# A second mixer with its order of work rewritten: scores ahead of a unit, convolution steps elsewhere, branch transposes spread out

## The reference, cut to what matters

```
proj = h @ w_in                       # 1024 x 7184: q, k, v, conv_in, gla_q/k/v/r, gla_lr, 3 x 1024 gates
sb_out   = stick_breaking_attention(q, k, v)      # 8 heads, 256 keys
   z = q k^T * scale;  log_keep = log_sigmoid(-z) on earlier keys
   w = exp(log_sigmoid(z) + reverse cumsum(log_keep) - log_keep);  out = w v
conv_out = silu(layer_norm(depthwise_conv_31(a * sigmoid(g)) + conv_b))   # 31 taps, 512 channels
gla_out  = rms_norm(gla_chunked(gla_q, gla_k, gla_v, log_alpha)) * silu(gla_r)
merged   = sum over the 3 branches of sigmoid(gate_b) * (branch_b @ w_branch[b])
out      = merged @ w_out
```

## Time and profile before

| | |
|---|---|
| median of 3 runs | 2477.34 us (2474.61 to 2477.43) |
| profiled execution | 2478.04 us, span of its instructions 2476.4 us |
| TensorE clock granted, mean | 0.97 of full speed |
| the mixers' stretches | from 1339 us on and from 2000 us on of the span |

### The profile page before, as it was taken

One profiled execution on the slowest core, in us unless ns is written; L12 is line 12 of the kernel. 1 busy time (PEld: TensorE's weight loads), 2 busy tenths in 40 slices (PEclk: granted clock), 3 DMA queues, 4 the chain that ended last, 5 costly groups with the idle time before them and its releaser, 6 DMA issues.

```text
span 2476.4 us, 38897 instructions
## 1 busy us (share of the span) xinstructions
PE 2310.3 (93%) x10840; PEld 1884.2 (76%) x10840; DVE 1754.4 (71%) x2364; ACT 1392.8 (56%) x1842; POOL 224.9 (9%) x291
## 2 busy tenths in 40 slices
PE   8988899998988899997999989999999998989998
PEld 6767788876776788875887777778878877777887
DVE  5767788886777788896556777665565559777555
ACT  4543677774653577774445555454454455654544
POOL 0000000000000000000000690000000009700000
PEclk9999999998999899998999999999999999999999
DMA  7433699994434699995665544555655554444652
GB/s 248 131 120 125 240 346 335 345 332 159 142 110 133 211 342 344 341 347 170 189 187 159 161 149 132 184 187 183 190 179 187 185 171 138 135 153 154 209 185 98
DMA packets 277483, 497.27 MB, mean 201 GB/s; under 512 B 20480, under 2 KB 112816, under 8 KB 277344
## 3 DMA queue, kind: packets, MB, share of 16 engines
q1 hardware_dynamic: 273296, 482.12, 58.2%
q0 software_dynamic: 4048, 13.50, 1.7%
HBM read 494.50 MB, written 1.05 MB: 200 GB/s over the span
## 4 chain that ended last, share of the span: by engine, by line
PE 72%; DVE 10%; DVEq 6%; ACT 4%; issue 4%; ACTq 1%; PEld 1%; DMA 1%; PEldq 0%; SPq 0%; POOLq 0%
PE g_bank L574 15%; PE g_bank L575 14%; PE g_bank L576 14%; PE s_bank L575 8%; PE s_bank L576 8%; PE s_bank L574 8%; DVE w_lo L563 2%; DVE conv_y L2456 2%; DVEq L2450 2%; ACT w_hi L558 1%; PE t_bank L1613 1%; PE t_bank L1757 1%; DVEq L2091 1%; DVE xt_lo L630 1%; DVE soft L2499 1%
## 5 line engine op out<-in xcount | busy, mean ns | idle before, releaser
L563 DVE TENSOR_TENSOR w_lo<-w_raw,w_hi 128x1024 fp32r<-128x1024 f32 x929 | 1114.5, 1229 | 397.6 <-ACT w_hi L558 369.3
L558 ACT ACTIVATE w_hi<-w_raw 128x1024 fp32r<-128x1024 f32 x929 | 965.8, 1058 | 489.6 <-PE g_bank L576 218.9
L574 PE MATMUL g_bank<-w_hi,xt_hi 128*128 128x512 f32 (+1 forms) x1152 | 467.6, 406 | 37.1 <-DVEq L635 12.6
L575 PE MATMUL g_bank<-w_lo,xt_hi 128*128 128x512 f32 (+1 forms) x1152 | 456.5, 396 | 0.0
L576 PE MATMUL g_bank<-w_hi,xt_lo 128*128 128x512 f32 (+1 forms) x1152 | 455.8, 396 | 0.0
L574 PEld LDWEIGHTS g_bank<-w_hi,xt_hi 128*128 128x128 f32 x1152 | 224.4, 195 | 93.5 <-issue 32.5
L576 PEld LDWEIGHTS g_bank<-w_hi,xt_lo 128*128 128x128 f32 x1152 | 223.1, 194 | 47.8
L575 PEld LDWEIGHTS g_bank<-w_lo,xt_hi 128*128 128x128 f32 x1152 | 224.4, 195 | 43.5
L574 PE MATMUL s_bank<-w_hi,xt_hi 128*128 128x512 f32 x640 | 252.7, 395 | 0.0
L576 PE MATMUL s_bank<-w_hi,xt_lo 128*128 128x512 f32 x640 | 249.8, 390 | 0.0
L575 PE MATMUL s_bank<-w_lo,xt_hi 128*128 128x512 f32 x640 | 249.3, 390 | 0.0
(11 more groups left out here) (333 smaller groups left out, 2666.0 us busy)
## 6 DMA issues: line engine op xcount, KB each, us to landing
w_raw<-in_w_in_dram SPq DMA_DIRECT2D x192, 512.0 KB, 4.6
w_raw<-in_moe_w_gate_dram SPq DMA_DIRECT2D x128, 512.0 KB, 5.3
w_raw<-in_moe_w_up_dram SPq DMA_DIRECT2D x128, 512.0 KB, 5.4
w_raw<-in_moe_w_down_dram SPq DMA_DIRECT2D x128, 512.0 KB, 5.4
w_raw<-in_ffn_w_gate_dram SPq DMA_DIRECT2D x176, 256.0 KB, 2.9
w_raw<-in_ffn_w_up_dram SPq DMA_DIRECT2D x176, 256.0 KB, 3.1
w_raw<-in_ffn_w_down_dram SPq DMA_DIRECT2D x88, 512.0 KB, 3.4
w_raw<-in_w_branch_dram SPq DMA_DIRECT2D x40, 512.0 KB, 4.0
```

Source lines behind the costliest of these rows:

```text
L558: nc.scalar.activation(half_of(w_hi, u, h), half_of(w_raw, u, h), ACT.Copy).then_inc(hi_ready, 1)
L563: nc.vector.tensor_tensor(half_of(w_lo, u, h), half_of(w_raw, u, h), half_of(w_hi, u, h).bitcast(F32), ALU.subtract).then_inc(lo_ready, 1)
L574: nc.tensor.matmul(dst, a_hi, b_hi, start=first, stop=False)
L575: nc.tensor.matmul(dst, a_hi, b_lo, start=False, stop=False)
```

## The change

Each group's scores and soft are issued one plain unit earlier (before the unit behind which stands the probs_t of the group before). Taps move: by the end of U18 it was 16 taps, it is 14; `alpha` is now followed by two taps instead of standing behind two; U20 to U24 carry 2, 3, 3, 3 and 4 taps, and the last tap is done with U24 instead of U25. `conv_back` and `conv_norm` come one unit earlier. The attention's transposes come behind U20 instead of U27, the GLA's behind U27, the convolution's between the halves of U29. The numbering of `t_bank` uses follows.

```diff
@@ -246,10 +246,10 @@
-    for i, (what, taps) in enumerate(((("lr", 0), 3), (("proj", 5), 1), (("proj", 6), 1), (("gate", 0), 1))):
-        group("scores", i)
-        group("soft", i)
-        take(taps)
+    group("scores", 0)
+    group("soft", 0)
+    for i, what in enumerate((("lr", 0), ("proj", 5), ("proj", 6), ("gate", 0))):
+        take(1)
         unit()
         hi()
         group("scan", i)
@@ -260,44 +260,46 @@
         lo()
         if i == 0:
             plain(1)
+        if i < 3:
+            group("scores", i + 1)
+            group("soft", i + 1)
         plain()
         group("probs_t", i)
-    plain(2)
+    plain()
     out("proj", 7)
     group("values", 3)
     step("alpha", n_t=2)
+    take(2)
     unit()
     step("alpha_end")
     hi()
     lo()
-    take(1)
+    take(2)
+    step("branch_t", n_t=2, j=0)
     step("gla_q", n_t=1)
-    plain(1)
+    plain(3)
     out("gate", 1)
     step("decay", n_t=2)
     step("k_dec")
-    plain(2)
+    plain(3)
     step("states", n_t=2, half=0)
     plain(3)
     out("gate", 2)
     step("states", n_t=2, half=1)
     plain(2)
-    take(2)
+    take(TAPS - done)
     step("gla_out", n_t=2)
-    unit()
-    hi()
-    lo()
-    take(2)
+    plain()
     out("gate", 3)
-    plain(TAPS - done)
     step("conv_back", n_t=2)
     plain()
     step("conv_norm")
     out("gate", 4)
-    step("branches_t", n_t=2)
+    plain()
+    step("branch_t", n_t=2, j=1)
     plain()
     out("gate", 5)
@@ -1371,13 +1372,15 @@
-                act_xt(t + T_AFTER_MIX2, 2, LATE_BRANCHES)
-                for k in range(6):
+                split_hi(u + 29, AHEAD)
+                act_xt(t + T_AFTER_MIX2, 2, BRANCH[2])
+                split_hi(u + 29, AHEAD + 1)
+                for k in range(1, 6):
                     ahead(u + 29, k)
@@ -1784,6 +1787,15 @@
+                def branch_quads(j, tj):
+
+                    a = ATTN2[BRANCH2_ORDER[j]]
+                    for tt in range(TT):
+                        bank = t_wait(tj + tt)
+                        for k in range(4):
+                            last = pe.transpose(bank[:, k * P:(k + 1) * P], proj[:, tt, a + k * P:a + (k + 1) * P], ident)
+                        last.then_inc(t_ready, 1)
@@ -1839,14 +1851,12 @@
+                    elif kind == "branch_t":
+                        if st["j"] == 0:
+                            pe.wait_ge(branch_ready, 4 * l + 4)
+                        else:
+                            pe.wait_ge(gla_ready, l + 1)
+                        branch_quads(st["j"], t + st["t"])
@@ -1915,20 +1925,11 @@
-                pe.wait_ge(gla_ready, l + 1)
-                pe.wait_ge(conv_ready, l + 1)
-                for i, (tt, j) in enumerate(LATE_BRANCHES):
@@ -1948,6 +1949,9 @@
                             last.then_inc(w_used, 1)
+                            if blk == 0 and j == 0 and h == 0:
+                                pe.wait_ge(conv_ready, l + 1)
+                                branch_quads(2, t + T_AFTER_MIX2)
@@ -2586,14 +2590,17 @@
-                dve_xt(t + T_AFTER_MIX2, At(16 * DEPTH + 10, (l, XT_LAYER2)), 2, LATE_BRANCHES)
+                split_lo(u + 29, AHEAD)
+                dve_xt(t + T_AFTER_MIX2, At(16 * DEPTH + 12, (l, XT_LAYER2)), 2, BRANCH[2])
+                split_lo(u + 29, AHEAD + 1)
                 dve.wait_ge(gate2_ready, 6 * l + 6)
```

More of the change, by code:

```diff
@@ L79 @@
 XT_LAYER2 = 22
-XT_ALL2 = 16
+XT_ALL2 = 17
 class At:
@@ L296, in plan_mixer2 @@
     out("gate", 4)
-    step("branches_t", n_t=2)
+    plain()
+    step("branch_t", n_t=2, j=1)
     plain()
     out("gate", 5)
-    assert next(units, None) is None and done == TAPS and t == 36 and g == 30 and s == S_MIX2
+    assert next(units, None) is None and done == TAPS and t == 38 and g == 30 and s == S_MIX2
     return steps, t
@@ L641, in build @@
         TILE = [[(tt, kq) for kq in range(2)] for tt in range(TT)]
-        EARLY_BRANCH = [(tt, 2) for tt in range(TT)]
-        LATE_BRANCHES = [(tt, j) for j in range(2) for tt in range(TT)]
+        BRANCH = [[(tt, BRANCH2_CHUNK[j] // 4) for tt in range(TT)] for j in range(3)]
         MERGED = [[(tt, blk) for tt in range(TT)] for blk in range(2)]
@@ L1322, in _ @@
                         act.drain().then_inc(probs_t2_ready, 1)
-                    elif kind == "branches_t":
-                        act_xt(t + st["t"], 2, EARLY_BRANCH)
+                    elif kind == "branch_t":
+                        act_xt(t + st["t"], 2, BRANCH[st["j"]])
                     elif kind == "conv_norm":
@@ L1373, in _ @@
                         act.drain().then_inc(gla_scaled, 1)
-                act_xt(t + T_AFTER_MIX2, 2, LATE_BRANCHES)
-                for k in range(6):
+                split_hi(u + 29, AHEAD)
+                act_xt(t + T_AFTER_MIX2, 2, BRANCH[2])
+                split_hi(u + 29, AHEAD + 1)
+                for k in range(1, 6):
                     ahead(u + 29, k)
                     if k == 4:
-                        act_xt(t + (T_AFTER_MIX2 + 4), 2, MERGED[0])
+                        act_xt(t + (T_AFTER_MIX2 + 2), 2, MERGED[0])
                 ahead(u + 35)
-                act_xt(t + (T_AFTER_MIX2 + 6), 2, MERGED[1])
+                act_xt(t + (T_AFTER_MIX2 + 4), 2, MERGED[1])
                 ahead(u + 36)
@@ L1930, in merged_quads @@
                     for tt in range(TT):
-                        bank = t_wait(t + (T_AFTER_MIX2 + 4 + 2 * blk + tt))
+                        bank = t_wait(t + (T_AFTER_MIX2 + 2 + 2 * blk + tt))
                         for j in range(4):
@@ L1939, in _ @@
                         s = uu.slot(RING)
-                        pe.wait_ge(xt_ready, XT_ALL2 * l + (2 * 9 + 9 + (j > 0)))
+                        pe.wait_ge(xt_ready, XT_ALL2 * l + (2 * 9 + 9 + j))
                         for h in range(2):
@@ L1969, in out_unit @@
                     return last
-                pe.wait_ge(xt_ready, XT_ALL2 * l + (2 * 9 + 11))
+                pe.wait_ge(xt_ready, XT_ALL2 * l + (2 * 9 + 12))
                 out_unit(0, 0, (0, 1))
@@ L1974, in _ @@
                 out_unit(0, 1, (0, 1))
-                pe.wait_ge(xt_ready, XT_ALL2 * l + (2 * 9 + 12))
+                pe.wait_ge(xt_ready, XT_ALL2 * l + (2 * 9 + 13))
                 out_unit(1, 0, (0,))
@@ L1979, in _ @@
                 out_unit(1, 1, (1,))
-                feed_forward(second, 2, 1, 12)
+                feed_forward(second, 2, 1, 13)
         @block.vector
@@ L2503, in _ @@
                         dve.drain().then_inc(log_w_ready, 1)
-                    elif kind == "branches_t":
-                        dve_xt(t + st["t"], At(16 * DEPTH + 8, (l, XT_LAYER2)), 2, EARLY_BRANCH)
+                    elif kind == "branch_t":
+                        dve_xt(t + st["t"], At(16 * DEPTH + 8 + 2 * st["j"], (l, XT_LAYER2)), 2, BRANCH[st["j"]])
                     elif kind == "values":
@@ L2595, in _ @@
                         k = 3 * blk + j
-                        ahead(u + 29, k)
+                        if k:
+                            ahead(u + 29, k)
                         unit_is_used(dve, u + (29 + k))
@@ L2610, in _ @@
                         if blk == 1 and j == 1:
-                            dve_xt(t + (T_AFTER_MIX2 + 4), At(16 * DEPTH + 14, (l, XT_LAYER2)), 2, MERGED[0])
+                            dve_xt(t + (T_AFTER_MIX2 + 2), At(16 * DEPTH + 14, (l, XT_LAYER2)), 2, MERGED[0])
                     dve.drain().then_inc(merged2_ready, 1)
                 ahead(u + 35)
-                dve_xt(t + (T_AFTER_MIX2 + 6), At(16 * DEPTH + 16, (l, XT_LAYER2)), 2, MERGED[1])
+                dve_xt(t + (T_AFTER_MIX2 + 4), At(16 * DEPTH + 16, (l, XT_LAYER2)), 2, MERGED[1])
                 ahead(u + 36)
```

## The result

Seven runs of the changed kernel have a median of 2486.26 us (2482.96 to 2488.44), seven of the kernel before 2475.11 us (2473.36 to 2477.43). The ratio is 1.0039, with a 95% interval of 1.0030 to 1.0049: slower by 0.4%, some 9.7 us by the ratio (the two medians lie 11.2 us apart). Forecast were 14.8 us more, 2492. The profiled execution took 2486.95 us; its span is 8.9 us longer than before.

The account below looks back on a forecast made before the run. TensorE, busy 93% of the span, was taken to bound the kernel. The five parts summed to +7.4 us per mixer, +14.8 for two; 2478.0 + 14.8 - 0.7 gave 2492 us, range 2468 to 2502.

Parts of the forecast that it names:

- A: Attention loop, scores and soft ahead of a plain unit: ACT's splits queue behind soft, U19 starts later; +5.7 us per mixer.
- B: Alpha ahead of its taps: its 3.2 us wait shrinks to 0.4 and U20's excess goes; -3.8 us per mixer.
- C: Attention transposes behind U20 fill both t_banks: gla_q waits 4.4 us, U21 pays 1.6; together +7.0 us per mixer.
- D: Three taps in U21 to U23: small waits at states (0.8) and 1.7 at gla_out; +2.7 us per mixer.
- E: Mixer's end: 13.0 us of waits and slow work go, 8.8 come, mostly gate banks for U27 and U29; -4.2 us.
- soft 1 to 3 each behind an idle wait of 3 to 5 us: Sign on ACT in the attention: idle 3 to 5 us before each soft, with hi splits right behind it.
- every new wait costs more than itself: Rule for TensorE's clock behind waits; if short waits cost only themselves, the sum is about 5 us less per mixer.
- splitting a wait saves nothing: Clock rule for TensorE: splitting one long wait into several short ones saves nothing, since re-warming is paid each time.
- the waits go and nothing replaces them: Rival: the three targeted waits vanish, half of 17 us net, -8.5 us per mixer, 2460 us; chance 0.14.
- within what can be told: Rival: attention loop costs 2, moved attention transposes 3, the rest pays for them; no telling change, 2477 us; chance 0.13.
- Worse than summed: Rival: attention waits push DVE back, the last tap is late again, +6 more per mixer, 2505 us; chance 0.03.

Follow-up runs that it names:

- e1: Kernel before with only scores and soft of group i+1 moved ahead of the plain unit; taps, alpha and transposes unmoved: 2493.36 us, ratio 1.0067.
- e2: Changed kernel with scores and soft of group i again just ahead of the unit behind which scan i stands: 2470.85 us, ratio to before 0.9976.
- e5: Changed kernel with, on ACT only, soft of group i+1 behind the plain unit's two splits instead of ahead: 2460.47 us, ratio 0.9935.
- e8: Kernel before with only the attention's order changed, scores ahead of the plain unit and its splits ahead of soft: 2465.49 us, ratio 0.9960.
- e3: Changed kernel with gla_q's transposes ahead of the attention's, nothing else: 2480.58 us, ratio 1.0017.
- e4: Changed kernel with 18 matmuls that nothing reads added behind the attention's transposes, in the wait for gla_q's bank: 2483.49 us, ratio 1.0033.
- e6: e5 with gla_q's transposes also put ahead of the attention's: 2454.95 us, ratio 0.9915.

## Why the prediction was right, and where its size was off

The direction and the mechanism hold; the sum was 7.4 us per mixer and the traces show 4.55 in the first and 3.3 in the second, from U10 to the next part. Another 1.0 of the 8.9 us lies behind the second mixer and in no term of the sum: a unit behind a wait of 2.41 us, the same in both traces, takes 7.02 us at clock 0.78 in the changed kernel and 5.58 at 1.00 before. Each part, from where the same step starts on TensorE in the two traces of the first mixer (the changed one enters U10 0.16 us later, which is taken off):

| part | forecast | measured |
|---|---|---|
| A, up to U19 | +5.7 | +5.5 (1476.20 against 1470.56) |
| B, up to the end of U20 | -3.8 | -4.5 |
| C, up to decay | +7.0 | +8.0 |
| D, up to U25 | +2.7 | +2.3 |
| E, up to the next part | -4.2 | -6.7 |

- **A** was read almost to the instruction: scan 3 at 1466.63 (forecast 1466.9), 3.4 us of wait at `values(0)` (3.6), 2.3 at `values(1)`, 2.9 at `probs_t(3)`. None came at `values(2)`. The sign "soft 1 to 3 each behind an idle wait of 3 to 5 us" holds for soft 1 (4.9) alone; soft 2 and 3 wait 2.2 and 2.9. DVE's waits for the splits behind them are 4.8, 3.5 and 4.8. e1 and e2 show it from both sides, 17 us with it alone and 15 without it; e5 and e8 show that it is ACT's order and not the early scores.
- **B**: alpha's wait is gone. e2 keeps it so.
- **C**: 4.5 us at L1889 (forecast 4.4), and U21 at 7.57 us, 2.0 above 5.57 (forecast 1.6); the four transposes of gla_q, at clock 0.50, take 0.4 more as well. e3 and e4 show both terms apart. The Trainium skill (TensorE: Matmul & The Clock Gate, section "HAM oscillation — how this bites in real kernels") tells of bursts of matmuls that each start at the lower clock after a wait. U21 agrees, at 0.72 behind its wait and at 1.00 with the wait filled; U29, at 1.00 behind 1.59 us, does not. That every new wait costs more than itself, and that splitting a wait saves nothing, was the prediction's own step from that section, and the rows do not bear it out.
- **D**: waits of 0.75 and 0.24 us at `states` and 0.92 at gla_out, where the forecast had 1.7. The remaining 0.4 is not clock, which is 1.00 in both places.
- **E** is the mis-sized term. What went is about as read, 12.9 us by difference (forecast 13.0). What came was put at 8.8 and is 6.2: conv_back 0.8, U27 2.3 with 1.6 of clock, U29 1.6 with none. The largest miss is U29, 1.6 instead of 4.0. PE's rows at conv_back, U27 and U29, and ACT's at the end of that chain:

```profile
1537.27 1.09 PE L1876 MATMUL t_bank<-const,conv_y 128*128 128x128 f32 x8 [0.77 <-DVEq L2463]
...
1546.09 0.59 PE L576 MATMUL g_bank<-w_hi,xt_hi 128*128 128x512 f32 x1 [2.26 <-ACT gate L1304]
...
1561.35 0.50 PE L576 MATMUL g_bank<-w_hi,xt_hi 128*128 128x512 f32 x1 [1.59 <-ACT gate L1304]
```

```profile
1553.18 1.06 ACT L1329 ACTIVATE proj<-proj 128x1024 f32<-128x1024 f32 x1 [1.43 <-DVEq L2543]
...
1560.61 1.27 ACT L1304 ACTIVATE gate<-g_bank,rstd_half 128x512 f32<-128x512 f32 x2
```

The chain from the last tap to the free bank is 24.2 us (1537.1 to 1561.3), not 25.0, and TensorE is there after 22.7, not 21.9, since U27 paid 1.6 for its clock. So the wait is 1.6 and not 3.1. U29 starts 24.1 us behind conv_back in both mixers of the changed kernel and of e2 to e6, whether U27 ran in 5.6 us or in 7.2; what U27 pays is taken off U29's wait. The prediction's sum has this rightly, with U27's clock inside its 21.9; so the 0.8 by which TensorE came later cost nothing. Measured against the chain, E was too high by 0.8 for its length, 0.9 for a clock that U29 did not pay, 0.4 at U30, where no wait is seen, and 0.4 for rounding. Two mixers of E are 5 us of the 5.9 between 14.8 and the 8.9 of the spans.

The errors of A to D (-0.2, -0.7, +1.0, -0.4) nearly cancel, which is luck. So is part of the clock's sum: forecast were 1.3, 1.6, 1.0 and 0.9 us for U19, U21, U27 and U29, 4.8 in all, and the first mixer has 0.9, 2.0, 1.6 and 0.1, the second 2.5, 1.6, 1.6 and 0.1.

The rival "the waits go and nothing replaces them" failed where it was said to, at ACT's program order. e5 takes 2460.5 us once that order is mended. That this is the rival's number is chance: e5 gains in the attention and still waits 5.6 us for gla_q. The rival "within what can be told" wanted the waits at `values` under 1 us; they are 3.4 and 2.3. "Worse than summed" wanted the last tap late again; conv_back waits 0.8.

## What to carry to other kernels

Before a step is issued earlier, list what stands behind it on each in-order engine: a step that still waits for another engine holds back every instruction behind it that could have run. Put the work that needs nothing (here weight splits) ahead of the one that waits. With two banks in turn, a pair of outputs early in the order also decides when the next step gets a bank. And price a wait with the clock behind it, unless the next wait ends at a time that another engine sets: there the slow stretch only shortens that wait.

## What the runs showed of the hardware

- The granted clock behind a wait can't be told from the wait's length alone. U27 behind 2.26 us ran at 0.76 (7.18 us) in the changed kernel and behind 2.25 us at 1.00 (5.58 us) in e3. U29's first half behind 1.59 us ran at 1.00, behind 3.19 us at 0.62. The same holds for 2.41 us behind the second mixer (5.58 us before, 7.02 changed). A forecast term of 1 to 2 us for the clock can be wrong by its whole size in a single place.
- Eighteen matmuls that nothing reads (4.39 us) in a wait of 4.5 us left 0.2 us of waiting and kept the next unit at clock 1.00 in both mixers, 2.0 and 1.6 us less.
